# A folded time transform, running sums on VectorE, a reciprocal in two, and gate work placed elsewhere

## The reference

```python
u = rms_norm(h, norm_w[l]) @ w_in[l]
f_in, f_gate, p_in, p_gate, c_q, c_kv, k_r, a_gate = jnp.split(u, split_idx, axis=-1)
y = jnp.fft.fft2(xf, axes=(1, 3), norm="ortho").real     # xf: f_in in 4 heads of 64; over time and channel
y = jnp.einsum('blhc,hcd->blhd', y, fourier_w)
...                                                       # pool: windows of 2, 4, 8, 16 tokens, one a group
s = cs[:, hi, g] - cs[:, lo, g]                           # running sum over the window
outs.append(s / cnt - xg[:, :, g])                        # mean less the value itself, then a 64x64 product
mix = jnp.concatenate([y_f * silu(f_gate), y_p * silu(p_gate), y_a * silu(a_gate)], axis=-1)
h = h + mix @ w_out[l]
```

## Time and profile before

| | us |
|---|---|
| median of 3 runs | 3553.79 |
| profiled execution | 3550.35 |
| its span (first to last instruction) | 3548.6 |
| PE / DVE / POOL / ACT busy | 3350.4 / 1653.1 / 936.9 / 767.2 |
| Fourier-and-pool stage, layer 0 / layer 1 | 66.08 / 64.51 |
| attentions' stage ahead of the first score | 19.2 |

### The profile page before, as it was taken

How to read it: one execution, slowest core, us unless ns; L and a number is a source line. 1 busy time by engine, 2 the same in 40 slices (tenths; PEclk the granted TensorE clock), 3 DMA queues, 4 the chain that set the end, 5 groups by cost and what they waited for, 6 DMA issues and landing times. The chain is left out here.

```text
span 3548.6 us, 41269 instructions
## 1 busy us (share of the span) xinstructions
PE 3350.4 (94%) x17666; PEld 2843.1 (80%) x17666; DVE 1653.1 (47%) x1968; ACT 767.2 (22%) x1080; POOL 936.9 (26%) x538
## 2 busy tenths in 40 slices
PE   8998999999899999999899999999998999999997
PEld 7986888999688898877768976676776788888885
DVE  3234664414366544129666555555855221212136
ACT  2112332102133310000122222544413110101012
POOL 2341001322400033335224312000333233333332
PEclk9999999999999999999999999999999999999998
DMA  3120000111100013342230004111531111111111
GB/s 122 42 72 23 25 1 18 63 47 50 54 10 18 7 42 138 106 126 75 90 133 25 1 33 116 45 43 35 207 128 39 40 50 51 48 48 48 48 48 59
DMA packets 69849, 210.85 MB, mean 59 GB/s; under 512 B 10352, under 2 KB 16112, under 8 KB 69524
## 3 DMA queue, kind: packets, MB, share of 16 engines
q1 hardware_dynamic: 65204, 191.97, 16.8%
q10 hardware_dynamic: 4464, 16.25, 1.2%
HBM read 166.17 MB, written 41.42 MB: 58 GB/s over the span
## 5 line engine op out<-in xcount | busy, mean ns | idle before, releaser
L196 POOL CAST w_hi<-w_raw 128x1024 fp32r<-128x1024 f32 x195 | 220.8, 1132 | 2318.5 <-PE psum L209 1683.0
L200 POOL TENSOR_TENSOR w_lo<-w_raw,w_hi 128x1024 fp32r<-128x1024 f32 x195 | 519.7, 2665 | 33.9 <-DVE x L1520 8.6
L209 PE MATMUL psum<-x,w_hi 128*128 128x512 f32 x1536 | 417.7, 394 | 12.4 <-POOL x L3033 10.0
L730 PE MATMUL psum<-h,w_hi 128*128 128x512 f32 x1024 | 336.8, 411 | 33.8 <-DVE gate_stage L757 21.7
L209 PEld LDWEIGHTS psum<-x,w_hi 128*128 128x128 f32 x1536 | 290.0, 189 | 79.0 <-issue 11.0
L730 PEld LDWEIGHTS psum<-h,w_hi 128*128 128x128 f32 x1024 | 193.8, 196 | 86.5 <-issue 24.2
L209 PE MATMUL psum<-x,w_lo 128*128 128x512 f32 x768 | 237.6, 391 | 0.0
L730 PE MATMUL psum<-h,w_lo 128*128 128x512 f32 x512 | 205.9, 402 | 0.0
L209 PE MATMUL psum<-hn_hi,w_hi 128*128 128x348 f32 x864 | 188.9, 327 | 15.6 <-DVE hn_lo L462 14.1
L209 PE MATMUL psum<-h,w_hi 128*128 128x512 f32 x736 | 197.0, 389 | 0.0
L209 PE MATMUL psum<-hn_lo,w_hi 128*128 128x348 f32 x864 | 185.1, 323 | 0.0
(11 more groups left out here) (427 smaller groups left out, 6292.3 us busy)
## 6 DMA issues: line engine op xcount, KB each, us to landing
w_raw<-in_w_mlp SPq DMA_DIRECT2D x64, 512.0 KB, 3.5
w_raw<-in_w_in SPq DMA_DIRECT2D x36, 512.0 KB, 3.5
w_raw<-in_w_gates SPq DMA_DIRECT2D x32, 512.0 KB, 3.8
gates_kept<-gate_stage SPq DMA_DIRECT2D x64, 256.0 KB, 2.1
gates<-gates_kept SPq DMA_DIRECT2D x32, 512.0 KB, 3.3
w_raw<-in_w_out SPq DMA_DIRECT2D x24, 512.0 KB, 3.5
w_raw<-in_w_branches_in SPq DMA_DIRECT2D x23, 512.0 KB, 3.5
proj_kept<-stage ACTq DMA_DIRECT2D x23, 512.0 KB, 2.6
```

What stands on the lines that cost most here:

```text
L196: self.core.nc.gpsimd.tensor_copy(self.hi[:, g % 2], self.raw[:, g % 2]).then_inc(self.hi_done, 1)
L200: self.core.nc.gpsimd.tensor_tensor(self.lo[:, g % 2], self.raw[:, g % 2], self.hi[:, g % 2].bitcast(F32), ALU.subtract) \
L209: last = nc.tensor.matmul(acc[:, c, :], w[:, g % 2, k, :], x(k)[:, c * ch:(c + 1) * ch], start=(k == 0 and part == 0), stop=(k == kt - 1 a ...
L730: last = nc.tensor.matmul(self.core.psum[:, self.bank(x // KT), :], one[:, g % 2, k, :], other(k)[:, c * CH2:(c + 1) * CH2], start=(k == 0 ...
```

## The change

- **Fold.** A real row's cosine sum over 1040 tokens needs only x[t] + x[1040 - t], its sine sum only the difference. New `InputRows.fold` makes these on VectorE, in place, right behind input tile 2. The first 521 columns then hold the sums and the last 519 the differences. The time transform takes 5 slices of 105 tokens instead of 10 of 104, each with its own cosine and sine rows; five tables are resident, each with its own semaphore.
- **Window sums.** GpSimd's work moves to VectorE in `input_products`, behind tiles 4, 5, 7, 8 and 9. Its buffers lie in slots that are written from tile 10 on; the counts come by two DMAs of SP.
- **Order on PE.** Pool heads first, then the first step, the transform of tile 0, that of tile 1, and the two Fourier heads. The even parts and the pieces of tile 0 are handled while PE works on tile 1.
- **Reciprocal.** Two halves of 1024 columns with a gate half between them.
- **Attentions.** The first gate tile uses both banks, with the value transposes behind it. Steps 24 to 27 have no gate pieces, steps 64 and 65 (which have no scores) have 4 each (`pieces`).
- **Gate loads.** SP waits for the stores of gate m ahead of the load of gate m.

```diff
-QT = 104
-NQ = L1 // QT
-KCH = 260
+QT = 105
+NQ = 5
...
+            sp.dma_start(rows.counts[1], io["inv_count"][:, 1, :]).then_inc(rows.counts_in[1], 16)
+            x.sync(sp, 1)
+            sp.wait_ge(x.var_ready, 1)
+            sp.dma_start(rows.counts[0], io["inv_count"][:, 0, :]).then_inc(rows.counts_in[0], 16)
+            x.sync(sp, x.n, 1)
...
+                if m == 2:
+                    for j in range(2):
+                        x.wait_read_out(dve, F_IN + j)
+                        rows.fold(j)
+                if m == 4:
+                    x.wait_read_out(dve, P_IN)
+                    rows.window_start(0)
+                if m == 5:
+                    rows.window_end(0)
+                if m == 7:
+                    x.wait_read_out(dve, P_IN + 1)
+                    rows.window_start(1)
+                if m == 8:
+                    rows.window_double()
+                if m == 9:
+                    rows.window_end(1)
...
-            sp.dma_start(inv, io["inv_count"]).then_inc(inv_loaded, 16)
+            for t in range(NQ):
+                sp.dma_start(tab[:, t, :], io["dft_time"][t]).then_inc(tab_in[t], 16)
             sp.dma_start(rope[:], io["rope"]).then_inc(rope_in, 16)
-            for t in range(NQ):
-                if t >= 2:
-                    sp.wait_ge(tab_used, t - 1)
-                sp.dma_start(tab[:, t % 2, :], io["dft_time"][t]).then_inc(tab_ready[t % 2], 16)
 
         @block.tensor
         def _(pe):
-
+            def head(tile, n, bank):
+                for c in range(NC1):
+                    last = nc.tensor.matmul(core.psum[:, bank + c, 0:CH1], bd[:, n, :],
+                                            slots[:, tile, c * CH1:(c + 1) * CH1], start=True, stop=True)
+                return last
+            for j in range(2):
+                head(P_IN + j, 2 + j, 2 + 3 * j).then_inc(pool_done, 1)
             for t in range(NQ):
                 if t >= 2:
                     pe.wait_ge(z_saved, t - 1)
                 for j in range(2):
-                    last = nc.tensor.matmul(core.psum[0:QT, t % 2, j * 256:(j + 1) * 256],
-                                            slots[:, F_IN + j, t * QT:(t + 1) * QT],
-                                            dft, start=True, stop=True)
+                    for part in range(2):
+                        c = (2 * j + part) * P
+                        t0 = first[part] + t * QT
+                        last = nc.tensor.matmul(core.psum[0:QT, t % 2, c:c + P], slots[:, F_IN + j, t0:t0 + QT],
+                                                dft[:, part, :], start=True, stop=True)
                 last.then_inc(z_done, 1)
 
             pe.wait_ge(z_saved, NQ)
-            for t in range(NQ):
-                pe.wait_ge(tab_ready[t % 2], 16 * (t // 2 + 1))
-                for j in range(2):
+            for j in range(2):
+                pe.wait_ge(pool_saved, j + 1)
+                for t in range(NQ):
+                    if j == 0:
+                        pe.wait_ge(tab_in[t], 16)
                     for part in range(2):
                         for half in range(2):
                             k0 = part * HALF + half * HA
                             last = nc.tensor.matmul(
                                 core.psum[:, 4 * j + 2 * part + half, 0:widths[half]],
-                                z[:, t, j, part, :], tab[:, t % 2, k0:k0 + widths[half]],
+                                z[:, t, j, part, :], tab[:, t, k0:k0 + widths[half]],
                                 start=(t == 0), stop=(t == NQ - 1))
-                last.then_inc(tab_used, 1)
-
-            pe.wait_ge(spectrum_ready, 8)
-            for j in range(4):
-                if j == 2:
-                    pe.wait_ge(pool_step, POOL_STEPS)
-                if j >= 2:
-                    pe.wait_ge(head_saved, j - 1)
-                src = F_IN + j if j < 2 else P_IN + j - 2
-                for c in range(NC1):
-                    last = nc.tensor.matmul(core.psum[:, 3 * (j % 2) + c, 0:CH1], bd[:, j, :],
-                                            slots[:, src, c * CH1:(c + 1) * CH1],
-                                            start=True, stop=True)
-                last.then_inc(head_done, 1)
+                last.then_inc(time_done, 1)
+
+            for j in range(2):
+                pe.wait_ge(spectrum_ready, 4 * j + 4)
+                head(F_IN + j, j, 3 * j).then_inc(head_done, 1)
...
-            act.wait_ge(tab_used, NQ)
             for j in range(2):
-                even = r[:] if j == 0 else mix[:, 0, :]
+                act.wait_ge(time_done, j + 1)
+                even = evens[:, j, :]
...
+    def fold(self, j):
+        v, x = self.core.nc.vector, self.slots[:, F_IN + j, :]
+        self.step(v.tensor_tensor(self.half, x[:, HALF:L1], x[:, HALF - 2:0:-1], ALU.subtract))
+        self.step(v.tensor_tensor(x[:, 1:HALF - 1], x[:, 1:HALF - 1], x[:, L1 - 1:HALF - 1:-1], ALU.add))
+        self.step(v.tensor_copy(x[:, HALF:L1], self.half))
+
+    def sum_pairs(self, dst, src, reach, half):
+        lo, hi = self.PAD - reach, self.PAD + L1 + reach
+        up = half if half > 0 else 0
+        self.step(self.core.nc.vector.tensor_tensor(dst[:, lo:hi], src[:, lo - max(half, 1):hi - max(half, 1)],
+                                                    src[:, lo + up:hi + up], ALU.add))
+
+    def window_start(self, j):
+        v, (a, b) = self.core.nc.vector, self.sums
+        self.step(v.memset(a[:, 0:self.PAD], 0.0))
+        self.step(v.memset(a[:, self.PAD + L1:], 0.0))
+        self.step(v.tensor_copy(a[:, self.PAD:self.PAD + L1], self.slots[:, P_IN + j, 0:L1]))
+        self.sum_pairs(b, a, 7, 0)
+        self.sum_pairs(a, b, 6, 1)
+
+    def window_double(self):
+        a, b = self.sums
+        self.sum_pairs(b, a, 4, 2)
+        self.sum_pairs(a, b, 0, 4)
+
+    def window_end(self, j):
+        v, (a, b) = self.core.nc.vector, self.sums
+        self.dve.wait_ge(self.counts_in[j], 16)
+        for rows, win in ((slice(0, 64), b), (slice(64, P), a)):
+            w, x = win[rows, self.PAD:self.PAD + L1], self.slots[rows, P_IN + j, 0:L1]
+            self.step(v.tensor_tensor(w, w, self.counts[j][rows], ALU.mult))
+            self.step(v.tensor_tensor(x, w, x, ALU.subtract))
...
-    dft_time = np.concatenate([np.cos(ph), np.sin(ph)], 1).reshape(NQ, QT, 2 * HALF)
+    dft_time = np.zeros((NQ * QT, 2 * HALF))
+    dft_time[:HALF, :HALF] = np.cos(ph[:HALF])
+    dft_time[HALF - L1:, HALF:] = np.sin(ph[HALF:])
+    dft_time = dft_time.reshape(NQ, QT, 2 * HALF)
...
-                for b in range(2):
-                    sp.wait_ge(self.gates.stored[b], 16 * N_GATES)
                 for m in range(N_GATES):
+                    for b in range(2):
+                        sp.wait_ge(self.gates.stored[b], 16 * (m + 1))
...
+    def pieces(i):
+
+
+        if i in range(WIDE, WIDE + 4):
+            return 0
+        return 2 if i < count else 4 if i < count + 2 else 0
...
-            gates.tensor(pe, KT)
+            gates.two = True
+            gates.tensor(pe, 2 * KT)
+            gates.two = False
             value_transposes(STICK, 0)
-            gates.tensor(pe, KT)
             pe.wait_ge(v_saved, 1)
             for i in range(count + 3):
                 if i < count:
@@ -1749,8 +1796,7 @@
                     if i >= 3:
                         output(i - 3)
                     value_transposes(*values[i])
-                if i < count:
-                    gates.tensor(pe, 2)
+                gates.tensor(pe, pieces(i))
...
-                if i % 4 == 3 and i < count:
+                if pieces(i) and sum(pieces(n) for n in range(i + 1)) % KT == 0:
...
-            link(nc.vector.reciprocal(mean, mean))
-            for _half in range(2):
+            for j in range(2):
+                link(nc.vector.reciprocal(mean[:, j, :], mean[:, j, :]))
                 gates.vector(dve)
...
```

More of the change, by code:

```diff
@@ L520, in wait_read_out, with input_products @@
         eng.wait_ge(self.core.weights.acc_free[g % 2], g // 2 + 1)
-def input_products(core, slots, hi, lo, h, vecs, r, tmp, ones, coming, comes_first, follows):
+def input_products(core, io, slots, more, hi, lo, h, vecs, r, tmp, ones, coming, comes_first, follows):
     nc = core.nc
@@ L1019, with __init__, step @@
-POOL_MAX = 16
-POOL_STEPS = 9 + 11
+                                        chunks(slots[:, F_GATE + j, :]), ALU.mult)
+class InputRows:
+    PAD = 8
+    def __init__(self, core, dve, slots, more, row_step, counts_in):
+        self.core, self.dve, self.slots, self.row_step, self.counts_in = core, dve, slots, row_step, counts_in
+        wide = flat(slots.early[:, CKV:, :])
+        width = L1 + 2 * self.PAD
+        self.sums = wide[:, 0:width], wide[:, width:2 * width]
+        self.counts = wide[:, 2 * width:2 * width + L1], more[:, HALF:HALF + L1]
+        self.half = more[:, 0:L1 - HALF]
+        self.done = 0
+    def step(self, ins):
+        self.done += 1
```

(4 more changed lines are left out.)

87 lines of the change are left out of this document (28 added, 59 removed).

## The result

The changed kernel took 3477.48 us (median of 4, 3474.6 to 3481.16) beside 3556.3 of the kernel before on the same chip: a ratio of 0.9779, 95% interval [0.9762, 0.9796]. In a later session it took 3481.39 (5 executions, 3479.03 to 3484.66), ratio 0.9797 [0.9783, 0.9811]. The nine have a median of 3480.3, against a forecast of 3480. Two executions of the same kernel differ by up to 10 us here, so terms of 1 to 6 us are read from traces, and the times only confirm the large ones. The profiled execution took 3480.07 us, span 3478.3: 70.3 us less than that of before.

The account below looks back on a forecast made before the run. TensorE was taken as the bound, busy 3350.4 of 3548.6 us. Terms of -61, -5.8, -4.0, -0.7 and +0.3 sum to -71.2 us: 3479.2 from the profiled 3550.35, forecast as 3480 us; 8-in-10 range 3467 to 3496.

Parts of the forecast that it names:

- Pool heads, 3.6 us: Fourier stage: six pool-head matmuls ahead of everything, scaled by columns to 0.61 us each at full clock, 3.6 us.
- First step, 5.6 us, of 4.9 to 6.9: Fourier stage: 20 matmuls of 128 columns with 105 stationary ones, 5.6 us taken between bounds from two other forms.
- Transform 18.2, tail 5.6, no table wait: Fourier stage: 40 transform matmuls 18.2 us; tail with second head and VectorE's product 5.6 us; five tables land in time.
- Layer 0, a 1.6 us remainder left in: Layer 0's Fourier stage takes 1.6 us more at lower mean clock; kept in its new stage, so 30.5 us gained.
- VectorE in the input products, 0: Input products: 26 added VectorE instructions per layer stay covered by idle time and two accumulators; cost 0 (0 to +2).
- Reciprocal, -5.8: RWKV branch: halving the reciprocal replaces TensorE's 6.07 us wait with waits of 1.4 and 0.5 to 1.3; -5.8 us.
- Two banks, -4.0: Attentions' start: a second bank removes the 2.93 us wait between half tiles; first score 4.0 us sooner (-3 to -4.5).
- Slices, -0.7 and +0.3: Gate work moved: steps 24 to 27, held by VectorE and ScalarE's chain, gain 0.7 us; the tail loses 0.3.
- The slow clock in the new stage: Rival: slow clock doubles two starts of 5 us work in the Fourier stages, plus 2 us in RWKV; +12, 3492 us, 10%.
- The moved gates free TensorE: Rival: the loop in steps 24 to 27 shortens as soon as TensorE is ahead; -5, 3475 us, 10%.
- The late table: Part of a rival: Fourier first step and transform slower than scaled, by stationary loads or late table; +3 to +6, 12%.
- VectorE as the bound: Rival: VectorE becomes the bound of the input products through the fold; 3580 us, slower than before, 1%.

Follow-up runs that it names:

- the kernel with the fold alone: Changed kernel with running sums back on GpSimd and pool heads at the Fourier stage's end, fold and five-slice transform kept: 3515.61 us, ratio 0.9893 to the kernel before.
- the kernels with three and six starts: Changed kernel with the first window's start (two memsets, copy, two sums) done three or six times behind input tile 4 of each layer: 3479.14 and 3498.56 us.
- the undone kernel: Changed kernel with the RWKV branch's reciprocal in one piece of 2048 again: 3481.03 us, ratio 0.9792 to the kernel before.
- the kernel with slices as before: Changed kernel with two gate slices in each of steps 0 to 63 and none behind them: 3477.81 us, ratio 0.9783 to the kernel before.

## Why the prediction was right

- **The sum, -71.2.** -70.3 by the traces. So close an agreement is in part luck: the Fourier stages gave 1.3 us more than forecast, the other terms 1.0 less, and stretches that no edit speeds up took 1.3 us more.
- **What bounds the kernel.** Right: all of the gain is matmuls gone or TensorE's waits gone, and where work was taken from a stretch with a second chain close behind (steps 24 to 27) it gave a fifth.
- **Pool heads, 3.6 us.** Mis-sized: 5.18. They have 3.68 us behind other matmuls, so the price by columns was right and the place was not: ahead of everything they pay a slow clock (0.71 over the first 5 us, in both layers). The old first step paid it in layer 0 only (10.75 us at 0.66 over its first 5 us, against 9.13 at 1.00 in layer 1), and layer 1 is the one that the sum was read from.
- **First step, 5.6 us, of 4.9 to 6.9.** Mis-sized the other way: 4.65, 0.233 us a matmul, just under the lower bound. I had taken a value between two forms; the one with the same streamed columns was the right scale. The two errors cancel: 9.8 us against 9.2.
- **Transform 18.2, tail 5.6, no table wait.** 17.89; 880.92 to 886.91 is 6.0; the waits are 0.69 and 0.47 against 0.9 and 0.4. No table was waited for: the fifth had landed 11.8 us behind the stage's start, near the 12 that I called the worst, and was wanted at some 17. The margin is not large for the first table: in the kernel with the fold alone, which has no heads ahead of the first step and loads the counts ahead of the tables, the transform waited 2.21 us for one in layer 0.
- **Layer 0, a 1.6 us remainder left in.** Wrong: the new stage takes 34.1 us in both layers at clock 0.96. The old remainder was the clock under the first step, 10.75 - 9.13 = 1.6 us.
- **VectorE in the input products, 0.** Right: no wait of TensorE there. The group of four 64-row operations took 7.0 us (bound 11.5; 18 if each had been held up for a whole split), as one was held up by GpSimd and three were not. The two-tile cover was shown by the kernels with three and six starts.
- **Reciprocal, -5.8.** -5.2 between the traces, 5.1 by the undone kernel. Waits of 1.49 and 1.09 where I had 1.4 and 0.5 to 1.3, with the clock at 1.00 behind both.
- **Two banks, -4.0.** -3.9, and up to 6 where the clock falls in the wait.
- **Slices, -0.7 and +0.3.** -1.0 and +0.9, a net of nothing, and in two of eleven traces 3.8 us worse than that. That the steps would hardly shorten was right, and so was the reason: a loop of 11.57 us for the 11.5 forecast. TensorE idle "for some 5 us" was not: 2.9 us, and the rest went into a slower clock, which I had not put in this term.
- **Gate loads, 0.** The first is issued 2.53 us ahead of the next phase's first matmul, before (2480.88, 2483.41) and after (2413.44, 2415.97). Behind that matmul the changed kernel takes 1062.3 and 1063.8 us; the other kernels take 1061.1 to 1067.3 and the one before 1065.2, so the -2.9 us of the table there can't be told from the spread.
- **The rivals.** The slow clock in the new stage did appear in its first 5 us, and is in the 34.1; it cost 1.5 us a layer, not 5. "The moved gates free TensorE" is excluded by the kernel with slices as before: the steps are 1.04 us shorter, not 5. The late table and VectorE as the bound did not happen.

## What to carry to other kernels

Before counting matmuls that a cheaper form saves, list what other engines do under them: here 43 us of GpSimd work had to leave the stage, or half of the saving stayed behind as a wait. A stretch in which TensorE shows no idle time can still have a second chain a microsecond behind; test it by the first few matmuls removed, and look at the clock as well as at the waits before filler work is taken out of a dense stretch. Price a group by its place as well as its form: the first group of matmuls of the Fourier stage ran 1.3 to 1.4 times as long (1.8 in two traces) where the clock was slow there, as it was in 26 of the 28 such stages traced.

## What the hardware showed that I had not expected

- Waits opened in a dense stretch were followed by a slower clock. With the slices out of steps 24 to 27 TensorE waits 0.73 and 1.25 us there, and all eleven such traces have the clock at 0.50 for a while (a mean of 0.57 over 4 us from 2224 in the changed kernel's first trace), and the three traces with the slices in place have 1.00 throughout.
- The same program differs by 10 us between executions (3474.6 to 3484.66), at mean clocks of 0.979 to 0.983.
- VectorE's copy of 128x1040 took 0.70 or 2.75 us, its fold sum of 128x519 0.70 or 2.78: the long ones began while a subtraction of GpSimd was running.
- The clock 20 us behind a stage differs between kernels, 0.84 or 1.00, with no edit near it; with six matmuls of that stage in another order it was at 1.00 in both layers of both traces.
